# Hybrid encoder step: the first two query tiles of a B head as one unit of attention work

## What is computed

```
def diff_weights(sc, lam):
    p = jax.nn.softmax(sc, axis=-1)
    p = p.reshape(p.shape[0], B_HEADS, 2, p.shape[2], p.shape[3])
    return p[:, :, 0] - lam * p[:, :, 1]

# diff_prompt, per block i of 128 queries:
q_chunk = (i * Q_BLOCK + jnp.arange(Q_BLOCK)) // CHUNK
sc = jnp.einsum('bqnd,bsnd->bnqs', qblk, k) * SCALE
sc = jnp.where(key_chunk[None, :] <= q_chunk[:, None], sc, NEG)
a = diff_weights(sc, lam)
return jnp.einsum('bhqs,bshe->bqhe', a, v)
```

## Time and profile before

| | us |
|---|---|
| median of 3 runs | 1033.09 (1032.91 to 1033.96) |
| the profiled execution | 1034.29 |
| its span, first to last instruction | 1032.5 |
| PE busy in the span | 1015.2 |
| DVE busy | 799.8 |
| ACT busy | 564.5 |
| POOL busy | 171.6 |

### The profile page before, as it was taken

The page is one execution under the profiler, slowest core; times in us unless marked ns, Lnnn a source line. Parts: engine busy times, 40 slices in busy tenths (PEclk is TensorE's granted clock), DMA queues, the critical chain, the costliest instruction groups (busy, mean ns, idle before and its releaser), DMA issues.

```text
span 1032.5 us, 19489 instructions
## 1 busy us (share of the span) xinstructions
PE 1015.2 (98%) x7600; PEld 989.2 (96%) x7600; DVE 799.8 (77%) x1222; ACT 564.5 (55%) x980; POOL 171.6 (17%) x296
## 2 busy tenths in 40 slices
PE   9999999999999999999999999999999999999996
PEld 9999999999999999988888899999999999999995
DVE  6998777888678895368767768698777788778884
ACT  6645554666456663345435646435654666555664
POOL 0000010010010035233544205000000010010023
PEclk9999999999999999999999999999999999999999
DMA  6436656656665536230112212316556656667542
GB/s 231 110 95 155 190 149 166 186 149 158 177 176 149 139 121 211 64 97 22 52 54 70 83 57 82 106 56 185 166 148 162 183 152 169 176 156 179 143 106 92
DMA packets 38890, 137.33 MB, mean 133 GB/s; under 512 B 5456, under 2 KB 8656, under 8 KB 38672
## 3 DMA queue, kind: packets, MB, share of 16 engines
q1 hardware_dynamic: 30736, 107.52, 30.1%
q0 software_dynamic: 8064, 28.58, 17.3%
HBM read 131.10 MB, written 4.98 MB: 132 GB/s over the span
## 4 chain that ended last, share of the span: by engine, by line
PE 51%; DVE 5%; issue 3%; ACT 1%; POOL 1%; DMA 1%; DVEq 0%; SPq 0%; ACTq 0%; POOLq 0%
PE acc L985 25%; PE acc L883 17%; PE acc L1120 3%; PE acc L1156 1%; PE acc L1226 1%; DVE w_lo L1853 1%; PE acc L1146 1%; DVE h_lo L1988 1%; DMA comb<-in_w2se 0%; POOL side L2520 0%; DMA raw<-in_w2se 0%; DVE res L2469 0%; POOL q_b L2500 0%; PE acc L1185 0%; PE acc L1189 0%
## 5 line engine op out<-in xcount | busy, mean ns | idle before, releaser
L985 PE MATMUL acc<-c_hi,w_lo 128*128 128x288 f32 x952 | 282.0, 296 | 0.0
L985 PE MATMUL acc<-c_hi,w_hi 128*128 128x288 f32 x952 | 281.0, 295 | 0.0
L985 PE MATMUL acc<-c_lo,w_hi 128*128 128x288 f32 x952 | 277.6, 292 | 0.0
L1853 DVE TENSOR_TENSOR w_lo<-raw,w_hi 128x1024 fp32r<-128x1024 f32 (+4 forms) x187 | 196.5, 1053 | 103.4 <-ACT w_hi L1332 87.5
L1332 ACT ACTIVATE w_hi<-raw 128x1024 fp32r<-128x1024 f32 (+4 forms) x157 | 140.7, 896 | 88.0 <-PE acc L985 57.3
L1502 ACT ACTIVATE comb<-acc 128x288 f32<-128x288 f32 x224 | 92.1, 411 | 167.3 <-PE acc L985 165.0
L985 PEld LDWEIGHTS acc<-c_lo,w_hi 128*128 128x128 f32 x952 | 180.8, 190 | 0.0
L985 PEld LDWEIGHTS acc<-c_hi,w_hi 128*128 128x128 f32 x952 | 179.0, 188 | 0.2 <-DVE w_lo L1853 0.2
L985 PEld LDWEIGHTS acc<-c_hi,w_lo 128*128 128x128 f32 x952 | 178.5, 188 | 0.0
L985 PE MATMUL acc<-h_hi,w_hi 128*128 128x288 f32 x574 | 170.8, 298 | 2.3 <-DVE h_lo L1988 0.8
L985 PE MATMUL acc<-h_hi,w_lo 128*128 128x288 f32 x574 | 169.8, 296 | 0.0
(11 more groups left out here) (257 smaller groups left out, 1831.4 us busy)
## 6 DMA issues: line engine op xcount, KB each, us to landing
raw<-in_w1st SPq DMA_DIRECT2D x17, 768.0 KB, 4.6
raw<-in_w2st SPq DMA_DIRECT2D x17, 768.0 KB, 4.3
raw<-in_w_qk SPq DMA_DIRECT2D x13, 512.0 KB, 3.7
raw<-in_w1sd SPq DMA_DIRECT2D x8, 768.0 KB, 4.2
raw<-in_w2sd SPq DMA_DIRECT2D x8, 768.0 KB, 4.3
raw<-in_w1gu SPq DMA_DIRECT2D x10, 512.0 KB, 4.6
raw<-in_w2gu SPq DMA_DIRECT2D x10, 512.0 KB, 3.8
raw<-in_w1st SPq DMA_DIRECT2D x9, 512.0 KB, 5.3
```

Of the source, the lines that this page charges most:

```text
L985: m = nc.tensor.matmul(acc[:, banks[side_of(p)], 0:HALF], w_part[:, col:col + P], x_part, start=n in (P1, P5, P2) and k == 0 and e == 0, s ...
L1853: return nc.vector.tensor_tensor(cols, src, hi.bitcast(FP32), ALU.subtract).then_inc(split_ready, 1)
```

## The change

The units ("B", h, 0) and ("B", h, 1) become one, which keeps the name ("B", h, 1). Its scores stand in one bank per map: tile 0 in columns 0 to 127, tile 1 in columns 128 to 383. It has one memset, two reduce_max and one scale, four exps, one normalise with two weighted sums, one round of three transposes, one copy of 384 columns, and three value products. There are 36 rounds. `FILL` from its 21st entry on, `SCORES_FIRST`, `ACT_LATE`, `ROOT_ROUNDS` and `HEAD_ROUNDS` are other tables; the number of filler steps is the same.

```diff
-FILL = (..., (0, 2), (0, 2), (4, 2), (0, 5), (3, 0), (1, 2), (3, 2), (4, 2), (2, 0), (3, 1), ...)
+FILL = (..., (0, 4), (3, 2), (1, 4), (3, 1), (1, 3), (3, 3), (2, 3), (3, 2), (0, 2), (2, 2), ...)
-        units += [("Bs", h, 0)] + [("B", h, i) for i in range(SEQ_TILES)] + [("L", h, 0)]
+        units += [("Bs", h, 0)] + [("B", h, i) for i in range(1, SEQ_TILES)] + [("L", h, 0)]
...
+        def query_tiles(i):
+            return (0, 1) if i == 1 else (i,)
+        def query_cols(i, tile):
+            first = P if (i, tile) == (1, 1) else 0
+            return first, first + (tile + 1) * P
...
-                        m = nc.tensor.matmul(acc[:, bank + e, 0:(i + 1) * P], q_b[rows, t % 2, i * P:(i + 1) * P],
-                                             k_b[rows, t % 2, 0:(i + 1) * P], start=True, stop=True)
+                        for tile in query_tiles(i):
+                            first, last = query_cols(i, tile)
+                            m = nc.tensor.matmul(acc[:, bank + e, first:last], q_b[rows, t % 2, tile * P:(tile + 1) * P],
+                                                 k_b[rows, t % 2, 0:(tile + 1) * P], start=True, stop=True)
...
-                    then(nc.vector.reduce_max(s[:, 0, 0:2], acc[:, bank:bank + 2, 0:(i + 1) * P], AX.X))
+                    for at, tile in enumerate(query_tiles(i)):
+                        first, last = query_cols(i, tile)
+                        then(nc.vector.reduce_max(s[:, 0, 2 * at:2 * at + 2], acc[:, bank:bank + 2, first:last], AX.X))
...
+                    for at, tile in enumerate(tiles):
+                        first, last = query_cols(i, tile)
+                        m = nc.vector.scalar_tensor_tensor(out=pr[:, first:last], in0=pr[:, BANK + first:BANK + last],
+                                                           scalar=s[:, 6, at:at + 1], in1=pr[:, first:last],
+                                                           op0=ALU.mult, op1=ALU.add)
```

More of the change, by code:

```diff
@@ L67 @@
 FILL_START = (1, 6)
[L68 removed]
+FILL = ((1, 0), (2, 0), (3, 0), (3, 0), (1, 4), (1, 0), (1, 0), (1, 0), (3, 0), (0, 3), (1, 0), (0, 0), (1, 0), (0, 3), (3, 0), (1, 1), (0, 3), (2, 1), (2, 0), (3, 3), (0, 4), (3, 2), (1, 4), (3, 1), (1, 3), (3, 3), (2, 3), (3, 2), (0, 2), (2, 2), (1, 1), (2, 1), (1, 2), (2, 2), (2, 3), (4, 9))
 ACT_SPLITS = (4, 0, 4, 0, 0, 0, 2, 1, 3, 0, 3, 0, 7, 2, 0, 7)
@@ L74 @@
 DVE_ROOTS = (1, 1, 1, 0)
-ROOT_ROUNDS = (1, 1, 1, 6)
-HEAD_ROUNDS = (2, 4, 3, 7)
+ROOT_ROUNDS = (1, 1, 1, 5)
+HEAD_ROUNDS = (2, 3, 3, 6)
 EARLY_BLOCKS = (1, 3)
 EARLY_FIRST = 3
-SCORES_FIRST = (2, 5, 8, 12, 15, 16, 17, 18, 19, 21, 24, 29, 31)
+SCORES_FIRST = (2, 5, 8, 12, 14, 15, 16, 17, 19, 21, 25, 27)
 V_BLOCKS = 4
-ACT_LATE = (2, 5, 6, 11, 14, 16, 18, 26, 29, 32, 33)
+ACT_LATE = (2, 5, 6, 11, 15, 17, 29)
 PERIODS = [("st", f) for f in range(PLAIN, PAIRED + 1)] + [("sd", 0, e) for e in range(KH)]
@@ L707, in head_values, with unit_width @@
             return slice(2 * HEAD * e, 2 * HEAD * e + HEAD)
+        def query_tiles(i):
[3 more added lines that the diff above has]
+            return first, first + (tile + 1) * P
+        def unit_width(i):
+            return query_cols(i, i)[1]
         def b_values(t):
@@ L1183, in transposes @@
                 elif kind == "B":
-                    for j in range(i + 1):
+                    for j in range(unit_width(i) // P):
                         m = nc.tensor.transpose(acc[:, T_BANK, j * P:(j + 1) * P], pr[:, j * P:(j + 1) * P], ident[:])
@@ L1224, in values @@
                 elif kind == "B":
-                    for j in range(i + 1):
-                        m = nc.tensor.matmul(acc[:, O_BANK, i * P:(i + 1) * P], pt[:, j * P:(j + 1) * P],
-                                             v_new[:, j, b_values(t)], start=j == 0, stop=j == i)
+                    for tile in query_tiles(i):
+                        first = query_cols(i, tile)[0]
+                        for j in range(tile + 1):
+                            m = nc.tensor.matmul(acc[:, O_BANK, tile * P:(tile + 1) * P],
+                                                 pt[:, first + j * P:first + (j + 1) * P],
+                                                 v_new[:, j, b_values(t)], start=j == 0, stop=j == tile)
                 else:
@@ L1712, in exps @@
                 elif kind == "B":
[L1713 to L1716, removed]
+                    for at, tile in enumerate(query_tiles(i)):
+                        first, last = query_cols(i, tile)
+                        for e in range(2):
+                            col = 2 * at + e
+                            m = nc.scalar.activation(pr[:, BANK * e + first:BANK * e + last], acc[:, bank + e, first:last],
+                                                     ACT.Exp, scale=SCALE, bias=st[:, par, 1, col:col + 1],
+                                                     accum_out=st[:, par, 4, col:col + 1])
                 else:
@@ L1730, in copy_turned @@
                 pt = probs_t[:, r % 2, :]
-                width = {"A": BANK, "As": 2 * P, "B": (i + 1) * P, "Bs": TOK_TILES * DEC}[kind]
+                width = {"A": BANK, "As": 2 * P, "B": unit_width(max(i, 1)), "Bs": TOK_TILES * DEC}[kind]
                 cols = slice(P if kind == "A" and i == 0 else 0, width)
@@ L2303, in maxima @@
                 elif kind == "B":
-                    then(nc.vector.memset(acc[0:CHUNK, bank:bank + 2, i * P + CHUNK:(i + 1) * P], NEG))
-                    then(nc.vector.reduce_max(s[:, 0, 0:2], acc[:, bank:bank + 2, 0:(i + 1) * P], AX.X))
+                    scored = acc[0:CHUNK, bank:bank + 2, :]
+                    if i == 1:
+                        scored = scored.rearrange("p b (q n) -> p b q n", q=2)[:, :, :, CHUNK:P]
+                    else:
+                        scored = scored[:, :, i * P + CHUNK:(i + 1) * P]
+                    then(nc.vector.memset(scored, NEG))
+                    for at, tile in enumerate(query_tiles(i)):
+                        first, last = query_cols(i, tile)
+                        then(nc.vector.reduce_max(s[:, 0, 2 * at:2 * at + 2], acc[:, bank:bank + 2, first:last], AX.X))
                 else:
@@ L2314, in maxima @@
                 else:
-                    cols = slice(0, 2 if kind == "B" else 1)
+                    cols = slice(0, 2 * len(query_tiles(i)) if kind == "B" else 1)
                     nc.vector.tensor_scalar(s[:, 1, cols], s[:, 0, cols], -SCALE, None, ALU.mult).then_inc(max_ready, 1)
@@ L2324, in normalise @@
                 dve.wait_ge(exp_done, sl + 1)
-                cols = slice(0, {"A": 4, "As": 1, "B": 2, "Bs": 1}[kind])
+                cols = slice(0, {"A": 4, "As": 1, "B": 2 * len(query_tiles(i)), "Bs": 1}[kind])
                 if kind[0] == "A":
                     then(nc.vector.tensor_tensor(s[:, 4, cols], s[:, 4, cols], s[:, 3, cols], ALU.add))
-                inv = inv_sum[:, t % 2, i, :] if kind == "B" else s[:, 5, cols]
+                inv = inv_sum[:, t % 2, query_tiles(i)[0]:i + 1, :].rearrange("p q e -> p (q e)") if kind == "B" else s[:, 5, cols]
                 then(nc.vector.reciprocal(inv, s[:, 4, cols]))
@@ L2338, in normalise @@
                 elif kind == "B":
[L2339 to L2343, removed]
+                    tiles = query_tiles(i)
+                    then(nc.vector.scalar_tensor_tensor(out=s[:, 6, 0:len(tiles)], in0=inv[:, 1:2 * len(tiles):2],
+                                                        scalar=lam[:, 4:5], in1=s[:, 4, 0:2 * len(tiles):2],
+                                                        op0=ALU.mult, op1=ALU.mult))
+                    for at, tile in enumerate(tiles):
+                        first, last = query_cols(i, tile)
+                        m = nc.vector.scalar_tensor_tensor(out=pr[:, first:last], in0=pr[:, BANK + first:BANK + last],
+                                                           scalar=s[:, 6, at:at + 1], in1=pr[:, first:last],
+                                                           op0=ALU.mult, op1=ALU.add)
                 else:
```

## The result

The changed kernel takes 1056.42 us (median of 4 runs, 1055.48 to 1057.75), the kernel before 1033.53 beside it (4 runs). The ratio is 1.0221 (95% interval 1.0208 to 1.0234): slower by 22.9 us. The forecast was 1051.1 with a range up to 1056.0, so the direction and most of the size were right, and the time lies 0.4 us above the range.

What follows compares the result with a forecast made beforehand. PE, busy 98%, bounds the kernel through its instruction stream and gaps. Boundary waits +19.4, old waits -0.7, PE work -1.0, restarts +0.3 gave +18.0 us: profiled 1052.3, median 1051.1, range 1040 to 1056.

Steps and rivals of the forecast that it cites:

- The boundaries: PE waits at filler block boundaries in the B heads, from block 9 to the middle of 16: 19.4 us together.
- the queue on DVE that I counted ahead of each take: DVE work such as maxima, normalise or low halves (1.15 each) delaying takes; PE then waits 1.57 us more.
- The joint unit's own worth: PE's own work in the four B heads: fewer narrow score groups and kind changes, taken as 1.0 us less.
- restarts: Filler runs resuming after four new stops cost 0.1 us more each for their first pair: +0.3 us.
- The clock: Rival, 18%: idle PE lowers the matmul clock once or twice, giving 1054.1 or 1057.1 us (range 1053 to 1058).
- two falls of 3.0 us, for the two waits of 4.3 and 4.0: Clock falls after the waits into block 13 (4.3) and at the middle of 16 (4.0), each costing 3.0 us.
- The sign that the prediction named for it: A granted clock below 1 around 575 or 625 would make it the clock's case.
- the 3.0 read from the warm-up: At program start 60 warm-up passes take 9.69 us against 6.7 at full clock: 3.0 lost per clock rise.
- the forecast's other two terms: PE's own work, 1.0 us less, and filler runs resuming after new stops, 0.3 us more.
- From the stretch to the median: Profiled execution forecast at 1052.3 us; its 1.2 excess over the median was taken off, giving 1051.1.
- DVE was not ahead of my count: Rival, 18%: DVE is free earlier at the boundaries, bare waits of 8.9 us; 1040.6 us, range 1040 to 1047.
- The joint units gave back: Rival, 6%: each merged round on PE frees a whole round's hand-overs, 4.8 us per head to balance at 1033.1 us.

Runs made afterwards that it cites:

- e4: Changed kernel with only DVE's order redone, four low halves of the weights moved behind the take or addition they preceded: 1049.08 us, ratio 1.0153.
- e3: Changed kernel with one filler step moved ahead of the last transposes, covering the middle of block 16: 1051.18 us, ratio 1.0171.
- e5: Kernel before with one filler step moved from round 27 to round 29, leaving the boundary into block 13 without cover: 1039.05 us, ratio 1.0055.
- e1: Changed kernel, joint units kept, placement tables redone so PE has round work at boundaries between filler blocks: 1032.13 us, ratio 0.9989 to the kernel before.
- e6: Kernel before, separate units, one filler step moved so every boundary from 9 to the middle of 16 falls one step late: 1075.38 us, ratio 1.0404.
- e2: Changed kernel plus spare PE matmuls in three waits: 10 at block 9, 17 at block 13, 16 at the middle of 16; 1051.56 us, ratio 1.0174.
- e8: Changed kernel with fewer spare PE matmuls: 3 at block 9, 9 at block 13, 8 at the middle of 16; 1052.60 us, ratio 1.0184.
- e7: e1 with block 10's low half of the weights moved behind the take of block 8 on DVE: 1032.90 us, ratio 0.9993 to the kernel before.

## Why the prediction was right on the waits and missed the size

**The boundaries: right.** 19.2 us were measured against 19.4. No boundary is off by more than 0.4, and the queue on DVE that I counted ahead of each take is what its timeline shows (two of them stand above). e4 moves only that queue and gets back the 1.2 per low half. e3 and e5 move one filler step each and get or lose one wait. That the layout makes the loss and not the joint unit is shown from both sides: e1 has the unit without the loss, e6 the loss without the unit.

**The joint unit's own worth: about as forecast.** I took 1.0 us for four heads. As the remainder of the stretch, less waits and falls, it comes out larger: 1.4 in e2 (19.2 - 0.95 of waits and 0.3 for restarts make 18.5, and the stretch is 17.1 above before, unrounded), and 1.6 in e1 (0.8 below before with 0.8 more of boundary waits). But a remainder takes in whatever else differs. Added up by kind from PE's starts, without idle time, e1 has 1.5 us less work than the kernel before: scores of B units 0.8 less (a joint group takes 0.86, from 573.45 to 574.31 above, which is the forecast's figure), transposes 0.2 less, value products the same, filler 0.8 less and scores of the sample units 0.2 more. The filler is less because e1 has it in 43 runs where the kernel before has 51. So the unit itself gave about 0.9, and the rest came with the layout.

**The clock: the step that failed.** The sum took PE's speed as unchanged. The clock stood among the rivals with 18%, as one or two falls of 3.0 us, for the two waits of 4.3 and 4.0. The sign that the prediction named for it came: the granted clock is 0.51 in 577.6 to 584.5 and in 628.8 to 635.7. Three things in that step were off:

- It was made a rival although my own sum had two waits of the length for which the earlier trace rows gave the warning. The reason against it was that the trace before shows no such idle stretch in mid-program. That trace had no case of it, so it spoke neither for nor against. The Trainium skill, TensorE: Matmul & The Clock Gate, section "Part 1: The HAM clock gate", has an idle array fall back to half its pulses. This case agrees in the main: 16 of 21 gaps of 2.3 us and more were followed by a fall, 5 were not.
- I counted only the waits of 4 us and more. The one at block 9 (2.5) was followed by a fall too.
- A fall costs 1.4 to 2.3 here (6.1 over three), not the 3.0 read from the warm-up. Part of the low stretch passes while PE still waits: in the window from 577.6 PE is busy for 5.2 of 6.9 us, and half of that would be 2.6, where 2.3 were measured.

With the measured waits and falls and the forecast's other two terms the sum reads 19.2 - 0.95 - 1.0 + 0.3 + 6.1 = 23.7, against a growth of the stretch of 23.2. The 0.5 between them is not assigned. The 0.3 for restarts is the prediction's estimate; no run measured it by itself.

**From the stretch to the median: two errors that cancel.** The stretch grew by 23.2 where 18.0 were forecast, 5.2 more. Outside it the changed kernel's trace is 1.6 shorter, which no term had. And I took off 1.2 from the profiled execution to the median, as for the kernel before, but the profiled execution of the changed kernel is 0.5 below its median: 1.7 more. So the median is 5.3 off, and that it is so near to the 5.2 is luck. The four runs of the changed kernel spread over 2.3 us, those of the kernel before over 1.2. That falls differ between executions of one kernel is what the mean clocks of e2 and e4 show; in the changed kernel the mean clocks (0.989 to 0.991) do not follow the times, so its spread stays unexplained.

**The other rivals.** DVE was not ahead of my count. The joint units gave back 0.2 to 0.4 per head, where 4.8 would have been needed for no loss.

## What to carry to other kernels

When work is laid out anew around a single buffer, list every point at which the busiest engine must wait for the buffer's release, and for each the work between and the queue ahead of the release. Here that list gave 19 us to within 0.3, and one step moved across such a point cost 5.7 us in e5 and gave back 5.2 in e3. If a listed wait of TensorE is over about 2 us, put a fall of its clock into the sum itself and not beside it as a risk: here 16 of the 21 waits of 2.3 us and more had one behind them, at 1.4 to 2.6 us each. Merging small units is worth little by itself (0.2 to 0.4 us each here), so a merge pays only if the layout around it is redone with it.

## What the hardware showed that I had not expected

- The granted clock fell behind gaps of 2.1 to 4.1 us, and not behind every gap of the same length: 2.3 us into block 10 was followed by a fall in two of the five kernels that keep that wait as it is in the changed one (after, e2, e3, e4, e8), and a gap of 3.5 in e6 by none.
- A fall may begin after PE is at work again: at 542.9 in e4, where PE had resumed at 542.4; at 629.0 in e8, where it had resumed at 628.3; at 529.3 in e4, where it had resumed at 527.8.
- Which waits are followed by a fall differs between executions of the same kernel: mean granted clock 0.998 in one execution of e2 and 0.995 in two others.
- Spare matmuls in a wait (34 passes of 128 columns at block 13) kept the clock at its upper level in the profiled execution of e2, and the next block started no later for them.
- A POOL operation on 128x96 elements, 0.39 us in most places, took 1.38 where DVE's low half of the weights ran beside it (e7, 528.03).
